# A norm's factor applied behind the products, features split a stage ahead, and a decay difference as a product, in a three-mixer transformer kernel

## The reference

```python
def rms_norm_2(x, g):
    xf = x.astype(jnp.float32)
    y = xf * lax.rsqrt(jnp.mean(xf * xf, axis=-1, keepdims=True) + RMS_EPS)
    return (y * g.astype(jnp.float32)).astype(x.dtype)

def swiglu(x, w_gate, w_up, w_down):
    return (jax.nn.silu(x @ w_gate) * (x @ w_up)) @ w_down
```

## Time and profile before

| | |
|---|---|
| median of 3 runs | 3176.68 us (3176.61 to 3178.8) |
| the profiled execution's own time | 3176.18 us |
| its span, first to last instruction | 3174.4 us |
| mean granted TensorE clock | 0.922 |
| TensorE busy | 2838.8 us, 89% of the span |
| VectorE | 1253.2 us, 39% |
| ScalarE | 846.6 us, 27% |
| GpSimd | 652.4 us, 21% |
| read from memory | 242.74 MB, 77 GB/s over the span |

### The profile page before, as it was taken

The page is one execution under the profiler, slowest core; times in us unless marked ns, Lnnn a source line. Parts: engine busy times, 40 slices in busy tenths (PEclk is TensorE's granted clock), DMA queues, the critical chain, the costliest instruction groups (busy, mean ns, idle before and its releaser), DMA issues. The chain is left out here.

```text
span 3174.4 us, 40429 instructions
## 1 busy us (share of the span) xinstructions
PE 2838.8 (89%) x16458; PEld 2250.0 (71%) x16458; DVE 1253.2 (39%) x1694; ACT 846.6 (27%) x1236; POOL 652.4 (21%) x457
## 2 busy tenths in 40 slices
PE   6977877768999889998978999999999888899998
PEld 4857733556888668887836788878888735678887
DVE  2346438734333343233235333333333356433323
ACT  2222122522121231222223322122221326332212
POOL 1001000312121131213064212123131220121312
PEclk7988976888999989999968999999999989999998
DMA  7300016012322223322201222323222220122231
GB/s 231 95 5 3 8 48 212 2 52 83 103 92 86 73 80 97 101 86 85 95 17 53 80 93 92 99 73 107 93 94 92 80 47 1 54 93 93 92 96 37
DMA packets 250871, 248.03 MB, mean 78 GB/s; under 512 B 20180, under 2 KB 246168, under 8 KB 250464
## 3 DMA queue, kind: packets, MB, share of 16 engines
q1 hardware_dynamic: 250514, 245.86, 24.6%
q10 hardware_dynamic: 206, 0.06, 0.0%
HBM read 242.74 MB, written 2.12 MB: 77 GB/s over the span
## 5 line engine op out<-in xcount | busy, mean ns | idle before, releaser
L276 DVE TENSOR_TENSOR ffn_wt_lo<-ring,ffn_wt_hi 128x2048 fp32r<-128x2048 f32 (+1 forms) x170 | 431.7, 2540 | 561.5 <-ACT ffn_wt_hi L269 561.2
L382 PE MATMUL bank<-ffn_feat_hi,ffn_wt_hi 128*128 128x512 f32 x1760 | 547.2, 392 | 29.6 <-DVE ffn_wt_lo L276 29.4
L382 PE MATMUL bank<-ffn_feat_lo,ffn_wt_hi 128*128 128x512 f32 x1760 | 545.3, 391 | 0.0
L382 PE MATMUL bank<-ffn_feat_hi,ffn_wt_lo 128*128 128x512 f32 x1760 | 544.9, 391 | 0.0
L269 ACT CAST ffn_wt_hi<-ring 128x2048 fp32r<-128x2048 f32 (+1 forms) x170 | 315.5, 1856 | 814.1 <-PE bank L382 813.9
L859 POOL TENSOR_TENSOR ffn_act_hi<-ffn_act,const 128x512 fp32r<-128x512 f32 x110 | 212.7, 1934 | 1265.3 <-DVE ffn_act L847 1265.3
L382 PEld LDWEIGHTS bank<-ffn_feat_hi,ffn_wt_hi 128*128 128x128 f32 x1760 | 332.7, 190 | 100.8 <-issue 25.4
L382 PEld LDWEIGHTS bank<-ffn_feat_lo,ffn_wt_hi 128*128 128x128 f32 x1760 | 333.0, 189 | 69.6
L382 PEld LDWEIGHTS bank<-ffn_feat_hi,ffn_wt_lo 128*128 128x128 f32 x1760 | 332.5, 189 | 69.5
L382 PE MATMUL bank<-ffn_act_hi,ffn_wt_hi 128*128 128x512 f32 x880 | 271.5, 390 | 0.9 <-POOL ffn_act_lo L861 0.9
L382 PE MATMUL bank<-ffn_act_lo,ffn_wt_hi 128*128 128x512 f32 x880 | 270.9, 389 | 0.0
(11 more groups left out here) (496 smaller groups left out, 3455.5 us busy)
## 6 DMA issues: line engine op xcount, KB each, us to landing
ring<-in_ffn_w_gate SPq DMA_DIRECT2D x44, 1024.0 KB, 5.3
ring<-in_ffn_w_up SPq DMA_DIRECT2D x44, 1024.0 KB, 5.3
ring<-in_ffn_w_down SPq DMA_DIRECT2D x32, 1024.0 KB, 5.2
ring<-in_ada_w SPq DMA_DIRECT2D x24, 1024.0 KB, 9.9
ring<-in_ffn_w_down SPq DMA_DIRECT2D x16, 768.0 KB, 4.4
ring<-in_w_ffn_gate SPq DMA_DIRECT2D x11, 1024.0 KB, 5.3
ring<-in_w_ffn_up SPq DMA_DIRECT2D x11, 1024.0 KB, 5.3
ring<-in_w_in SPq DMA_DIRECT2D x8, 1024.0 KB, 5.3
```

What stands on the lines that cost most here:

```text
L276: self.nc.vector.tensor_tensor(self.wl[:, n % 2, 0:words], K.ring[:, n % RING, 0:words], self.wh[:, n % 2, 0:words].bitcast(F32), ALU.subt ...
L382: lasts[m] = pe.matmul(outs[m], a, b, start=n == 0 and p == 0, stop=end and p == 2)
```

## The change

Four things are changed.

1. *Features ahead.* A stage that completes x (`ahead`) also makes, for the first six of the eight tiles, the square, x * gain as high part (both ScalarE) and its low part (VectorE): the next stage's split features without the norm's factor (class `Ahead`). They lie in tensors that outlive the stage (`K.fh`, `K.fl`). GpSimd adds the squares.
2. *The factor behind the products.* The next stage (`defer`) splits the first chunk of weights in four pieces and starts its products; it makes tiles 6 and 7 of the features itself. In front of the last feature tile TensorE sums the squares by one product of 512 columns, ScalarE takes the root of 128 x 512 numbers and VectorE the reciprocal (`K.rs`). In the FFN each gate product is multiplied by it before SiLU and SiLU's outcome once more behind it (for the up product); in plain stages it is multiplied in when a tile leaves its bank. The last norm is applied to the output, one number per token. The FFN's loops are written out. This concerns six stages: ffn2, ab_in, ffn3, ffn4, mla_in, ffn5, and the end. FFN 1, mixer 1 and the first restart keep their norms.
3. *The decay difference as a product.* F[t] - F[s] comes from a second product with 40 rows per head, added in the score's bank; the copies of -F and GpSimd's bias go.
4. *Side products.* The forget gate's product (ab_in) and the rope part (mla_in), plain float32 products behind the others, become split products between the others.

```diff
+class Ahead:
+    DONE = KD - 2
+    def __init__(self, K, st, gain, exact=False):
+        self.K, self.gain, self.exact = K, gain, exact
+        self.s_sq, self.s_hh = st.sems("next_squared", "next_high")
+    def scalar(self, k):
+        K = self.K
+        if k < self.DONE:
+            K.nc.scalar.activation(K.h[:, k, :], K.x[:, k, :], ACT.Square).then_inc(self.s_sq, 1)
+            dst = K.fx[k] if self.exact else K.fh[:, k, :]
+            K.nc.scalar.mul(dst, K.x[:, k, :], self.gain(k)).then_inc(self.s_hh, 1)
+    def vector(self, dve, k):
+        K = self.K
+        if k < self.DONE and not self.exact:
+            dve.wait_ge(self.s_hh, k + 1)
+            K.nc.vector.scalar_tensor_tensor(K.fl[:, k, :], K.x[:, k, :], self.gain(k), K.fh[:, k, :].bitcast(F32), ALU.mult, ALU.subtract)
+    def add(self, pool):
+        K = self.K
+        for k in range(1, self.DONE):
+            pool.wait_ge(self.s_sq, k + 1)
+            K.nc.gpsimd.tensor_tensor(K.h[:, 0, :], K.h[:, 0, :], K.h[:, k, :], ALU.add)
+            pool.drain()
 class Split:
...
+        if n == self.pieces:
+            for j in range(4):
+                part = slice(j * words // 4, (j + 1) * words // 4)
+                last = self.nc.scalar.copy(self.wh[:, n % 2, part], K.ring[:, n % RING, part]).then_inc(self.s_wh, 1)
+            act.drain().then_inc(K.high_done, 1)
+        else:
+            self.nc.scalar.copy(self.wh[:, n % 2, 0:words], K.ring[:, n % RING, 0:words]).then_inc(K.high_done, 1)
...
+        elif self.defer:
+            for k in range(Ahead.DONE, KD):
+                self.nc.scalar.mul(self.hh[:, k, :], K.x[:, k, :], self.defer(k)).then_inc(self.s_hh, 1)
+            for k in range(Ahead.DONE, KD):
+                self.nc.scalar.activation(K.h[:, k, :], K.x[:, k, :], ACT.Square).then_inc(self.s_sq, 1)
+    def features_deferred(self, dve):
+        K, v = self.K, self.nc.vector
+        a, b = Ahead.DONE, KD - 1
+        for k in (a, b):
+            dve.wait_ge(self.s_hh, k - a + 1)
+            v.scalar_tensor_tensor(self.hl[:, k, :], K.x[:, k, :], self.defer(k), self.hh[:, k, :].bitcast(F32),
+                                   ALU.mult, ALU.subtract).then_inc(self.s_hl2 if k % 2 else self.s_hl, 1)
+        dve.wait_ge(self.s_sq, 2)
+        v.tensor_tensor(K.h[:, a, :], K.h[:, a, :], K.h[:, b, :], ALU.add)
+        dve.drain()
+        v.tensor_tensor(K.h[:, 0, :], K.h[:, 0, :], K.h[:, a, :], ALU.add).then_inc(self.s_add, 1)
+    def deferred_sum(self, pe):
+        K = self.K
+        pe.wait_ge(self.s_add, 1)
+        pe.matmul(K.bank[7][:, :], K.k("ones"), K.h[:, 0, :], start=True, stop=True).then_inc(self.s_sum, 1)
+    def deferred_root(self, act):
+        K = self.K
+        if self.defer:
+            act.wait_ge(self.s_sum, 1)
+            K.nc.scalar.activation(K.rs[:, :], K.bank[7][:, :], ACT.Sqrt, bias=K.k("eps")[:, 0:1], scale=1.0 / D).then_inc(self.s_root, 1)
+    def deferred_inverse(self, dve):
+        K = self.K
+        if self.defer:
+            dve.wait_ge(self.s_root, 1)
+            K.nc.vector.reciprocal(K.rs[:, :], K.rs[:, :]).then_inc(self.s_rs, 1)
+            dve.drain()
     def normed_vector(self, dve):
...
+        if wait and self.defer:
+            if k % 2 == 0:
+                pe.wait_ge(self.s_wl, k // 2 + 1)
+            if k == KD - 1:
+                self.deferred_sum(pe)
+            if k >= Ahead.DONE:
+                pe.wait_ge(self.s_hl2 if k % 2 else self.s_hl, 1)
...
+                        if c == 0:
+                            S.deferred_root(act)
...
+                                if defer:
+                                    act.wait_ge(s_gate, i + 1)
+                                    nc.scalar.activation(g[:, m, :], g[:, m, :], ACT.Silu).then_inc(s_silu, 1)
...
+                        elif r % 2 == 0 and defer:
+                            dve.drain()
+                            for m in range(2):
+                                dve.wait_ge(K.tiles_done, plan.tile(name, c, m))
+                                v.tensor_tensor(g[:, m, :], K.bank[m][:, :], K.rs[:, :], ALU.mult).then_inc(s_gate, 1)
+                            for m in range(2):
+                                dve.wait_ge(s_silu, i0 + r + m + 1)
+                                v.tensor_tensor(g[:, m, :], g[:, m, :], K.rs[:, :], ALU.mult)
...
+    def go(bank, engine):
+        rs = K.rs[0:bank.shape[0], 0:bank.shape[1]]
+        return v.tensor_tensor(dst, bank, rs, ALU.mult) if scale is None else v.scalar_tensor_tensor(dst, bank, scale, rs, ALU.mult, ALU.mult)
+    return go
...
+    def forget():
+        S = box["split"]
+        pe.wait_ge(box["root"], 1)
+        pe.wait_ge(box["wl"], 1)
+        product3(pe, K.bank[7][0:8, :], (((box["hi"][:, k, :], box["lo"][:, k, :]), S.feature(pe, k, False)) for k in range(KD))).then_inc(box["pe"], 1)
...
+                        for n in (2 * j, 2 * j + 1) if decay else ():
+                            h, i = items[n]
+                            a, b = decay(h, i, width(n))
+                            pe.matmul(K.bank[n % 4][:, 0:width(n)], a, b, start=False, stop=True).then_inc(s_score, 1)
...
-        def prep(pool, out, h, i):
-            w = (i + 1) * P
-            nc.gpsimd.tensor_scalar(out, B.nF[:, h, 0:w], B.F[:, 8 * i + h:8 * i + h + 1], None, ALU.add)
-            pool.drain()
-            return nc.gpsimd.tensor_tensor(out[:, w - P:w], out[:, w - P:w], K.k("causal")[:, T - P:T], ALU.add)
...
+                        bias=lambda h, i: K.k("causal")[:, 384 - i * P:384 - i * P + (i + 1) * P],
+                        decay=lambda h, i, w: (B.fq[d(h), h // 2, i * P:(i + 1) * P], B.fk[d(h), 0:w]))
+    out_stage(K, "ab_out", lambda k: y[:, k, :], True, ahead)
...
+            residual_norm(K, "post2", lambda i: coef[:, 32 + i:33 + i], gain("norm_ffn_2"))
+            ffn_stage(K, "ffn2", True, defer=gain("norm_ffn_2"), ahead=gain("norm_mix_2"))
+            mixer2(K, gain("norm_mix_2"), gain("norm_ffn_2", 8))
+            ffn_stage(K, "ffn3", True, defer=gain("norm_ffn_2", 8), ahead=gain("norm_ffn_2", 16))
+            ffn_stage(K, "ffn4", True, defer=gain("norm_ffn_2", 16), ahead=gain("norm_mix_2", 8))
+            mla_in_stage(K, B3, gain("norm_mix_2", 8))
```

559 lines of the change are left out of this document (319 added, 240 removed).

## The result

The changed kernel takes 3119.11 us (median of 4 executions, 3114.80 to 3122.45); the kernel before took 3176.64 beside it (3174.62 to 3178.80, 4 executions). The ratio is 0.9823, 95% interval 0.9809 to 0.9837: 57.5 us less, where 72.6 were predicted. That lies in the stated range of 3090 to 3124, but outside the forecast's own 3097 to 3111. The profiled execution took 3117.26 us, its span is 3115.4 (before 3174.4, so 59.0 less), and the mean granted clock 0.934. TensorE is busy for 2794.1 us, 90% of the span, VectorE for 1380.9, ScalarE for 836.5, GpSimd for 551.9.

What follows compares the result with a forecast made beforehand. TensorE at full speed bounds the five FFNs, about 1,800 us; only gaps between stages and stages where TensorE isn't full can shrink. 44.6 + 5.6 - 5.1 + 1.3 + 6.2 + 7 + 13 = 72.6 off 3176.7 gives 3104 us, range 3090 to 3124.

Steps and rivals of the forecast that it cites:

- restarts give less: Rival: barrier, semaphores or late features 6 and 7 cost 2 us in each of six restarts; 3116 us, chance 0.14.
- fox doesn't gain: Rival: in the fox attention a three-engine chain or TensorE becomes the bound; 3117 or 3131 us, chance 0.15.
- Five restarts, post2: Shorter gaps at five stage borders save 44.6 us; the restart behind post2, which keeps its norm, saves 5.6.
- The sum in TensorE's stream: One fp32 product of 512 columns in each of six stages, 0.87 us each, costs 5.1 us.
- The FFN's chain at nothing: VectorE's four more operations per gate-and-up pair: about 7 us hidden behind 10.9; cost 0, first pair under a microsecond spare.
- ab_in: End of ab_in: forget product as 24 split products in the middle instead of behind everything; saves 1.3 us.
- The end: From last product to end of span: 23.1 us become 16, as transposes no longer wait for the norm; saves 7.
- mla_in: End of mla_in: rope as split products with a tail of about 6.4 us; 36.2 becomes 30.0, saves 6.2.
- Part 1: Prediction's restart term: sum, root and reciprocal run during the next stage's first products; five restarts save 44.6 us.
- The fox attention: Fox attention: GpSimd's biases become 32 more products of 40 rows; 66 us become 53, saves 13.
- The clock at 0: Half clock behind restarts stays, so 0 gained; the rival, clock holds over short gaps, gives 12 us more, chance 0.13.
- Unchanged code at 0: Nothing gained or lost, 0 us, in stages whose code stays the same.

Runs made afterwards that it cites:

- e3: Changed kernel with ScalarE loading the square-root table in output stages without waiting for x[6] and x[7]; 3111.4 us.
- e6: Changed kernel with the first chunk of weights of each of the six deferring stages split whole instead of in four pieces; 3134.9 us.
- e7: Changed kernel with four more unused 128x512 VectorE products per pair in the four deferring FFNs; 3115.4 us.
- e4: Changed kernel with mla_in reordered on VectorE: rope-weight subtraction ahead of the reciprocal, key rotation ahead of the last tile's evacuation; 3107.1 us.
- e1: Changed kernel without the decay products in the fox attention, causal mask kept; 3111.8 us.
- e9: Changed kernel with unused TensorE products filling its waits in the fox prep stage and the fox attention; 3110.8 us.
- e2: Changed kernel with GpSimd making the fox attention's bias again, prep stage as in the kernel before; 3121.9 us.
- e13: e12 plus unused TensorE products ahead of the fox attention, in each fox and MLA attention round, and at the end of each FFN; 3068.1 us.
- e12: e10 plus GpSimd's window sums, their four products and evacuation moved from the fox prep stage to beside the fox attention; 3082.7 us.
- e10: Changed kernel with the early square-root table, the reordered mla_in and the first weight chunk split in eighths together; 3096.6 us.
- e5: Changed kernel with one unused 512-column TensorE product at the end of stages completing x and one at the start of deferring stages; 3119.8 us.

## Why the prediction was right, and where not

The direction, the range and most of the forecast's mechanism were right; the sum was 13.6 us too high against the spans. By its number alone the result fits the rivals at 3116 (restarts give less) and 3117 (fox doesn't gain) better than the forecast at 3104. The gaps exclude the first; the second is true in part. The shortfall is fox 5.5, mla_in 3.7, unchanged code 3.7 and FFNs 1.0; the other terms differ by less than 1.5 each.

- *Five restarts, post2* (48.9 of 50.2): right. The gaps of 3.3 and 2.9 us were 2.9 and 4.0: smaller behind FFNs, because the border took less, larger behind output stages, because the table load was missed. It stands in the diff as one line behind the loop; what was not looked at is what that loop waits for last. e3 shows it: 1.5 us each. e6 shows the worth of the four pieces.
- *The sum in TensorE's stream* (-5.1): right, -4.5 in four FFNs for a predicted 3.5. What the other 1.0 is was not traced.
- *The FFN's chain at nothing*: right, and the margin of "less than a microsecond" was in truth at least 1.7 (e7).
- *ab_in*: right. *The end*: 8.4 for 7.
- *mla_in* (+6.2): this step failed. The prediction added up products and a tail and left out what the product of the rope weights waits for. Part 1 says that a reciprocal of 3.35 us comes in on VectorE; that the subtraction of these weights is queued behind it was not drawn from it. The wait of 2.76 us and the half clock behind it, some 1.6 more, are nearly all of the miss: the stage's 35.8 us are 4.6 above 31.2, the 30.0 of the prediction and 1.2 more to the sums. e4 takes that order back and in the same edit shortens the tail by 4.4, 9.0 us in all.
- *The fox attention* (+13, "I take 53"): this step failed in its size, 7.5 measured. The work came out right by luck (43.5 us of full clock predicted, 42.6 measured): the decay products are 7.5, not 11.2, and the rest is 35.1 (e1), not 48.85 x 0.66 = 32.2. The mean clock of 0.66 over a stretch that runs partly at one half and partly at full is the likely reason that both came out wrong. What failed is the assumption about the clock: the prediction scaled from MLA at 0.93; the stretch ran at 0.86, and at 0.50 in its first 6 us. With 42.6 / 0.93 + 8.5 of idle time it would be 54.3, an estimate, so the clock is some 3.7 of the missing 5; the rest is the step from 54.6 to 53, for which no row was given. e9 gives 52.9 us at 0.97. Against the rival the prediction held that a busy TensorE gets its clock back; the 14.0 us of products with 8 rows, at 0.50 throughout, are a row of the kernel before that says otherwise. The rival "fox doesn't gain" is neither fully true nor excluded: with GpSimd's bias the stretch took 65.5 and 64.5 (e2), without it 58.0 to 63.3.
- *The clock at 0* (+12 for the rival): right for the change as it is, behind gaps of 2.84 to 4.02 us. At 2.48 and 2.0 us behind output stages it held in each case seen; at 2.37 behind ffn3 it fell in 2 of 3.
- *Unchanged code at 0*: the MLA attention lost 3.1 us. That this isn't the change is argued from its spread: over the 13 profiles in which its code is the same (all but e13's) it took 99.5 to 104.2, in rounds of 11.8 us at full clock and 13.4 where a piece at half clock fell into one; the changed kernel without the decay products (e1) had 99.6. This belongs in the range, and there was no row for it, since one profile shows one draw.

## What to carry to other kernels

When work is moved into a stage, list for every engine what is queued behind the new instruction and who waits for it, also in stages where the new instruction itself is harmless; and ask what the last wait of each engine's program is, since the border waits for it. A stretch with a clock below 1 should be predicted with the clock of its own beginning: what TensorE did just ahead of it counts. And an engine that a change leaves idle is the place to put what still stands alone on the path: e12 got 14 us out of a GpSimd that part 3 had freed. Where the same code takes 58 us in one profile and 63 in the next, one profile before and one after don't price an edit in it.

## What the hardware showed that was not expected

- The same idle time doesn't always have the same effect on the clock. Ahead of ffn4, 2.84 to 2.86 us of idle were followed by some 3.4 us at 1.2 GHz in 7 of 7 profiles, 2.37 us in 2 of 3. Ahead of ffn3 and ffn5, 2.47 and 2.48 us (e3) and 1.99 to 2.00 us (e10, e12, e13) were followed by 2.4 GHz in 8 of 8, but idle pieces of 1.74 and 0.33 us (e5) by a drop. Behind ffn3 in the changed kernel and in e1, e10 and e12, and behind mla_out in the changed kernel, the drop began 0.6 to 1.1 us after the restart, when TensorE was busy again (behind ffn4 in the changed kernel within 0.4); an FFN is 1.6 us longer for it. What decides within these is open.
- Being busy isn't enough for the clock: 14.0 us of back-to-back products with 8 rows (kernel before, 1610.54 on) left it at 0.50, and the stretch behind them began at 0.50. The fillers that e9 and e13 put into that stage have 128 rows, and the stretch behind them began at 1.00. Whether it is the rows that decide was not tried by itself.
- Products whose outcome nobody reads are worth their place: e9's 14 fillers took 5 us out of a stretch of 58.
- 21 us of GpSimd beside the attention (e12) made VectorE's multiplication from SBUF to SBUF 1.7 times as long (383 to 652 ns) and left the operation that reads a PSUM bank alone.
